# GpSimd's remainder of a weight piece as two instructions of half its columns, in a two-part transformer on one core

## The reference

```
x = x + 0.5 * swiglu(norm(x), w_in, w_out)          # 1024 -> 2*2816 -> 1024
x = x + merged(branch_1, branch_2, branch_3) @ w_out
x = x + 0.5 * swiglu(norm(x), w_in, w_out)
```

## Time and profile before

| | |
|---|---|
| median of 3 runs | 2648.29 us (2648.15 to 2649.47) |
| the profiled execution | 2648.21 us, its span 2646.3 us |
| TensorE busy (matmuls) | 2609.3 us, 99% of the span |
| GpSimd busy | 2033.4 us, 77% |
| ScalarE busy | 1286.5 us, 49% |
| VectorE busy | 862.4 us, 33% |
| granted clock of TensorE | 0.998 of the full one |
| read from HBM | 469 MB, 178 GB/s over the span |

### The profile page before, as it was taken

How to read it: one execution, slowest core, us unless ns; L and a number is a source line. 1 busy time by engine, 2 the same in 40 slices (tenths; PEclk the granted TensorE clock), 3 DMA queues, 4 the chain that set the end, 5 groups by cost and what they waited for, 6 DMA issues and landing times.

```text
span 2646.3 us, 48214 instructions
## 1 busy us (share of the span) xinstructions
PE 2609.3 (99%) x19726; PEld 2392.2 (90%) x19726; DVE 862.4 (33%) x1518; ACT 1286.5 (49%) x1910; POOL 2033.4 (77%) x906
## 2 busy tenths in 40 slices
PE   8999999999999999999999999999999999999998
PEld 6999999899899989989989999998998989898897
DVE  2644364211232336411121133733122132473212
ACT  4444555444444555544444445745444444574443
POOL 7888666788888856688888886468888878537886
PEclk9999999999999999999999999999999999999999
DMA  6566544555656654655555556255556556525553
GB/s 232 184 199 200 185 135 134 192 186 189 205 182 194 202 181 135 168 192 188 186 195 189 177 187 211 97 167 189 187 183 197 189 168 199 184 97 177 192 188 136
DMA packets 128738, 474.79 MB, mean 179 GB/s; under 512 B 14432, under 2 KB 14432, under 8 KB 127520
## 3 DMA queue, kind: packets, MB, share of 16 engines
q1 hardware_dynamic: 124704, 454.09, 52.4%
q0 software_dynamic: 3840, 17.83, 2.3%
HBM read 469.24 MB, written 2.62 MB: 178 GB/s over the span
## 4 chain that ended last, share of the span: by engine, by line
PE 92%; DVE 4%; ACT 1%; DMA 1%; issue 1%; POOL 0%; DVEq 0%; SPq 0%; ACTq 0%; POOLq 0%
PE psA L379 52%; PE psY L379 38%; PE psT L430 2%; DMA ring<-in_weights 1%; DVE psY L1277 0%; POOL rest L1063 0%; PE psT L652 0%; DVE psY L1265 0%; DMA cst<-in_consts 0%; DVE st L1362 0%; DVE x L1292 0%; ACT upper L1874 0%; DVE arena L1664 0%; ACT xT_upper L1874 0%; ACT G L1905 0%
## 5 line engine op out<-in xcount | busy, mean ns | idle before, releaser
L1063 POOL TENSOR_TENSOR rest<-ring,upper 128x1024 fp32r<-128x1024 f32 (+1 forms) x834 | 1993.1, 2409 | 549.5 <-ACT upper L1874 538.8
L1874 ACT ACTIVATE upper<-ring 128x1024 fp32r<-128x1024 f32 (+1 forms) x834 | 870.5, 1052 | 801.6 <-DMA ring<-in_weights 800.7
L379 PE MATMUL psA<-xT_rest,upper 128*128 128x256 f32 x2784 | 390.6, 283 | 0.0
L379 PE MATMUL psA<-xT_upper,upper 128*128 128x256 f32 x2784 | 388.9, 282 | 0.6 <-ACT arena L1874 0.6
L379 PE MATMUL psA<-xT_upper,rest 128*128 128x256 f32 x2784 | 383.5, 280 | 0.0
L379 PEld LDWEIGHTS psA<-xT_upper,upper 128*128 128x128 f32 x2784 | 364.0, 189 | 14.0 <-ACT arena L1874 1.3
L1318 DVE TENSOR_TENSOR psA<-sil,psA 128x256 f32<-128x256 f32 x144 | 61.8, 429 | 955.4 <-ACT sil L1874 955.3
L379 PEld LDWEIGHTS psA<-xT_rest,upper 128*128 128x128 f32 x2784 | 359.1, 192 | 0.0
L379 PEld LDWEIGHTS psA<-xT_upper,rest 128*128 128x128 f32 x2784 | 352.6, 189 | 0.0
L379 PE MATMUL psY<-upper,hT_rest 128*128 128x512 f32 x704 | 205.3, 397 | 0.0
L379 PE MATMUL psY<-upper,hT_upper 128*128 128x512 f32 x704 | 203.8, 394 | 0.0
(11 more groups left out here) (282 smaller groups left out, 2993.6 us busy)
## 6 DMA issues: line engine op xcount, KB each, us to landing
ring<-in_weights SPq DMA_DIRECT2D x862, 512.0 KB, 3.6
G<-in_rows POOLq DMA_DIRECT2D x6, 1024.0 KB, 8.4
G<-in_rows POOLq DMA_DIRECT2D x7, 512.0 KB, 6.0
arena<-rel_by_distance POOLq DMA_DIRECT2D x8, 256.0 KB, 7.6
x<-in_x SPq DMA_DIRECT2D x2, 512.0 KB, 5.8
par<-in_params POOLq DMA_DIRECT2D x4, 256.0 KB, 6.2
xn<-in_mem POOLq DMA_DIRECT2D x1, 1024.0 KB, 11.8
memory_transposed<-arena POOLq DMA_DIRECT2D x1, 1024.0 KB, 5.4
```

The costliest lines, as they stand in the source:

```text
L379: i = pe.matmul(out, lhsT, rhs, start=start, stop=stop)
L1063: pool.tensor_tensor(rest[:, r, 0:n], ring[:, r, 0:n], upper[:, r, 0:n], ALU.subtract)\
L1874: act.activation(out, in_, func, **kw).then_inc(*up)
```

## The change

GpSimd's split of a piece issues two subtractions, the first on columns 0 to n/2, the second on columns n/2 to n. The wait for ScalarE's signal stays in front of the first. The first raises a new semaphore, "rest begun", for which nobody waits; the signal that TensorE waits for is raised by the second. Nothing else of the kernel is touched.

```diff
                 pool.wait_ge(*sig["upper parts"].after(("piece", h)))
                 r, n = h % R, width(h)
-                pool.tensor_tensor(rest[:, r, 0:n], ring[:, r, 0:n], upper[:, r, 0:n], ALU.subtract)\
+                m = n // 2
+                pool.tensor_tensor(rest[:, r, 0:m], ring[:, r, 0:m], upper[:, r, 0:m], ALU.subtract)\
+                    .then_inc(*sig["rest begun"].up())
+                pool.tensor_tensor(rest[:, r, m:n], ring[:, r, m:n], upper[:, r, m:n], ALU.subtract)\
                     .then_inc(*sig["rest parts"].up(("piece", h)))
```

## The result

The changed kernel took 2658.68 us (median of 7 runs, 2655.37 to 2670.35), the kernel before beside it 2648.51 (7 runs, 2647.57 to 2654.99). The ratio is 1.0037 with a 95% interval of 1.0027 to 1.0047: slower by 10 us, where +0.7 was forecast. The profiled execution took 2655.37 us, 7.2 more than the one that the prediction was made from.

What follows compares the result with a forecast made beforehand. TensorE, busy 2609.3 of 2646.3 us, was taken to bound the kernel. Costs of 2.7 us less 2.0 coming back gave +0.7 on 2648.3, so 2649.0 us; range 2646.0 to 2653.0.

Steps and rivals of the forecast that it cites:

- What comes back: VectorE operations held by whole remainders get in sooner beside halves, mainly before TensorE's gap at 2303: -2.0 us in the sum.
- four rivals: Costlier second instruction, chance 0.10; larger VectorE gain, 2643 us at 0.03; new wait at a power, 0.15; program not as described, 0.01.
- Rival 3: With dearer halves or overrated slack at 1141, a second norm's power makes TensorE wait: +3.5 us, 2651.8 us; chance 0.15.
- The price c: Fixed cost of one more GpSimd instruction a piece: 0.13 us, near bounds 0.08 and 0.19; 108 us more GpSimd work.
- Rival 1: The second instruction costs more than its columns at 834 places, 0.29 us or more: 2654 to 2673 us, slower; chance 0.10.
- estimate of 0.35 us: Fixed part of a GpSimd subtraction by the skill's cycle figures: +7 us by the formula, 2655 us or more, slower.
- (a), the start: Three remainders in a row from 15.03 us delay TensorE's weight load at 23.05: 0.40 us.
- (b), late pieces: Seven pieces, from 231 to 2284 us, whose remainder ends right before TensorE uses it: 0.65 us.
- (c), the norm at 1141: Second layer's feed-forward norm: its power queues behind 16 remainders on GpSimd, so VectorE's scaling and the transposes come 1.1 us late.
- that part costs nothing as long as that idle time lasts: In the feed-forward, 48 pieces' extra 6.2 us fit into GpSimd's 16.8 us idle; densest 40 us, 2.2 into 2.45.
- 2.0 as the most: Gain at TensorE's gap at 2303 behind VectorE's shift and sums: 1.0 us sure, 2.0 the most, 1.5 taken.
- The signs: Expected: 1668 subtractions, GpSimd near 2140 us, shorter 2303 gap; wrong if halves last 1.4 us, feed-forward idle grows or gap stays.

Runs made afterwards that it cites:

- experiment 9: Changed kernel with a 78 ns hole between halves only in pieces feeding the first feed-forward of both first-kind layers, and six behind: 2645.20 us, ratio 0.9985.
- experiments 2: Changed kernel with halves only in the second kind of layer, one subtraction a piece in the first kind: 2645.23 us, ratio 0.9983.
- experiment 4: Changed kernel with GpSimd waiting for its own first half before the second, a 78 ns hole in every piece: 2652.95 us, ratio 1.0009.
- experiment 8: Against the kernel before: four quarters for each piece of the second kind of layer, whole pieces in the first: 2693.85 us, ratio 1.0170.
- experiments 3: Changed kernel with the second subtraction of each piece taking 32 columns and the first all the others: 2658.38 us, ratio 1.0027.
- 10: Changed kernel with subtractions of 544 and 480 columns instead of two of 512: 2658.02 us, ratio 1.0032.
- (5): Changed kernel with an already met wait ahead of each second half, the halves still touching: 2658.49 us, ratio 1.0035.
- experiment 1: Changed kernel with VectorE's three four-column operations of step 0 of `bounds` made as twelve of one column: 2652.70 us, ratio 1.0011.
- experiment 6: Changed kernel with halves only in the first kind of layer, whole pieces in the second: 2664.60 us, ratio 1.0053.

## Why the prediction was wrong

**The step that failed** is in "What comes back": "With halves such a waiter gets in after 1.2 us where it came in the first half, and gains nothing where it came in the second." That a waiter gets in at the next end of a subtraction was read from the kernel before, where 88 of 89 did, and carried over to a queue where it isn't so. 98 of 107 still did; the other nine were kept out, the longest for 23 us. Its companion, "Most of these waits hide, for TensorE has other work", was true for waits of 2 us, and was never asked of longer ones. The term that the sum lacks is +9.0 us in the profiled execution: 1.7 and 4.6 of waiting and 2.7 of slow clock. The clock's part, too, has no term in the prediction. With the hole put only at those places, it goes, and with it the whole loss (experiment 9). None of the four rivals held it. Rival 3 was a new wait, but at a power in GpSimd's own queue; a new wait for VectorE was the one that the prediction's own mechanism pointed at.

The prediction had a hint in hand. The first of the three operations lasted 3.95 us at 67.03 in the kernel before, VectorE's timeline:

```profile
67.03 3.95 DVE L1515 TENSOR_TENSOR arena<-par 128x4 f32<-128x4 f32 x1
```

A remainder ended 1.5 us into it, and it let the next one of 2.4 us go first: the one of 89 that missed a hand-over. It was not among the rows read.

**The price c** was right. The sixteen halves from 726.69 to 745.45 us start 1.251 us apart, a pair takes 2.50 against the 2.366 of the earlier trace rows, c = 0.14 where 0.13 was taken. Rival 1 (c at 0.29 or more) is out; its outcome, slower, came by another way, so the 0.11 given to it is no credit to the prediction. The prediction's estimate of 0.35 us sets the 4497 ns of the Trainium skill, GPSIMD Engine Reference, section "Elementwise — side-by-side cycle accounting", against this case's 2426 ns. It is not borne out: the measured c is 0.14.

**(a), the start:** 0.40 forecast, 0.55 found (matmul at 23.05 before, 23.60 after), of which TensorE was 0.14 late before the place. **(b), late pieces:** 0.65 forecast; the places can't be read singly. About 1625 the changed kernel loses 1.2 us, but experiments 2 and 9, with the same halves there, lose 0.1 and 0.2, so that is not c alone. **(c), the norm at 1141:** 1.1 forecast. In the changed kernel it doesn't show, since TensorE came 10 us late and the power had time. In the kernel with the hole in part it shows by itself, from 1.2 to 2.5 us late; the power, VectorE's scaling and the transposes there, against the earlier trace rows:

```profile
1144.39 0.57 POOL L1043 TENSOR_TENSOR st<-st,cst 128x1 f32<-128x1 f32 x1
1145.07 1.42 DVE L1258 SCALAR_TENSOR_TENSOR xn<-x,st,G 128x512 f32<-128x512 f32 x2 [2.66 <-POOL st L1043]
...
1145.87 1.32 PE L430 MATMUL psT<-cst,xn 128*128 128x128 f32 x8 [1.03 <-DVE xn L1258]
```

That is 1.3 us for 1.1. With c at 0.26 (experiment 4) the same run of pieces costs 3.6 from 860 to 1142 and 1.5 at the norm, so "that part costs nothing as long as that idle time lasts" holds for 0.14 and no longer for 0.26.

**What comes back** was too small: 2.0 forecast in the sum, with "2.0 as the most" at 2303. Found in the changed kernel: 2.1 us for the wait at 2303, 1.5 for the matmuls behind it and 1.1 at 1640, 4.7 in all. TensorE's timeline after, where the earlier trace rows had 2.0 us idle in front of the same matmuls:

```profile
2310.34 1.98 PE L379 MATMUL psY<-arena,PT 128*128 128x512 f32 x4
2312.25 0.71 PE L379 MATMUL psA<-arena 64*128 64x128 f32 x8
```

The bound was set with "since TensorE's idle time is all there is", and that is a second step that failed. In the kernel before, the clock falls behind this wait of 2.0 us; the window behind it in the kernel before, and that with the same matmuls in the kernel after:

```profile
2304.40:2307.80 3.40, 3.40 (x18) 3.40 (x17) 3.19 (x8) 3.09 (x11) 0.00 (x0) 0.50 0.03 5
```

```profile
2313.20:2316.60 3.40, 3.40 (x40) 3.26 (x39) 2.94 (x7) 3.40 (x11) 0.00 (x0) 1.00 0.02 5
```

At 0.50 eight matmuls of 256 columns take 2.07 us and the next eight 1.82, in the kernel after 1.22 and 1.12. That is the gain behind the wait: without the wait the clock doesn't fall. At 1640 TensorE idled 0.84 us for ScalarE's `Sc` in the kernel before and doesn't in the kernel after, which is most of the 1.1 there. Were it not for the operations kept out, the changes at c = 0.14 would come to about -3 us in the trace and -4 by medians (experiment 9), still within 0.2%. The gains are thus larger than the costs, so that the forecast of +0.7 would have had the wrong sign even then, and by the medians the time would lie below the range's lower end of 2646.0.

**The signs.** Of what the profile was to show, the number of subtractions (1668), their length (1.31 us) and GpSimd's busy time (2150.6 for 2140) came true, and so did the shorter gap at 2303; the line that was wrong was "VectorE's longest waits for a remainder at 1.2 us where they were 2.1 to 2.4". None of the three signs that were to prove the forecast wrong came up, apart from 0.7 us more idle time behind a remainder at the start, which the forecast had counted. All three asked after GpSimd's subtractions or the gap at 2303, none after VectorE.

## What to carry to other kernels

When an engine's long instruction is cut into short ones that follow each other without a hole, don't count on others getting in at every joint: ask of each VectorE operation that contends with GpSimd what would be late if it were kept out to the end of GpSimd's run, and put a short wait between the pieces, or leave them whole, where the answer is TensorE. A wait of TensorE can be paid again, when its clock falls behind it; the same holds for a wait that a change takes away. And where a kernel's single runs suddenly spread over 10 or 20 us, compare the longest instructions of one kind in two profiles before averaging.

## What the runs showed of the hardware

- A VectorE operation of 128x4 with both inputs in SBUF was kept out by touching GpSimd subtractions for 7.7 to 20.6 us; one of 128x1024 for 23 us, 18 halves, in most kernels. It is not only operations with two inputs: the copy of 128x56 in experiment 8 took 22.3 us, and a scaling of 128x4 took 5.9 us at 839.20 in the changed kernel. With a hole of 78 ns at every second joint it happened to none of 105 that were blocked, with one subtraction a piece to none of 89, and in experiment 9 only outside the pieces with a hole. The Trainium skill, SBUF — State Buffer, section "Who interferes with whom", says that the port pair that VectorE and GpSimd share is an exclusive lock, that a VectorE instruction with two SBUF inputs contends with a GpSimd instruction that reads SBUF, and that issue order decides who blocks. The trace agrees for the instruction that is running: the operations of the earlier trace rows end with the remainder that was running. Read as an order of service it doesn't hold: at 728.88 VectorE's operation was there ahead of 14 halves and each of them went first.
- What decides whether a waiting operation gets in at a touching joint is open. It isn't an even rhythm (experiments 3 and 10), nor the lack of a wait on the second half (5). When the operation comes has a part in it: in the seven profiles with touching halves of 512 columns, of the blocked ones that came in the first 0.6 us of a half with another touching it, 11 of 321 were still waiting when the next had begun, of the later ones 36 of 84. The second share is somewhat too high, for an operation that comes in the last 0.2 us and gets in at the joint isn't counted as blocked. These are often the same operations in each kernel, so it may be something else about them. Why whole remainders, which touch too, kept nobody out for three or more is open as well; with subtractions of 992 and 32 columns (3) it does happen, so the length of one is not all of it.
- The one-column form with a scalar from SBUF took 0.20 to 0.22 us beside running subtractions and was never blocked; the four-column operations that it replaces took 0.16 alone.
- After 4.4 us (changed kernel) and 7.05 us (experiment 1) without matmuls TensorE's granted clock was at 0.50, for 5.9 and 4.3 us of the work behind them by the windows' means, worth 2.7 and about 2 us of lateness on top of the wait. It also fell behind the 2.04 us at 2303 in the kernel before. It stayed at 1.00 behind the 1.56 us at 84.40 in the changed kernel, and behind a wait of 2.05 us at 1667 in experiment 6, so the length of the wait alone doesn't tell.
